# Normalising before the split, statistics by halves, and PSUM read directly: a two-layer encoder on one core

## What is computed

```python
def rms_norm(x, g):
    y = xf * lax.rsqrt(jnp.mean(xf * xf, axis=-1, keepdims=True) + EPS)
    return (y * g).astype(x.dtype)

def conv_ffn(h, w_up, conv_w, conv_b, w_down):
    z = causal_dwconv(h @ w_up, conv_w, conv_b)      # width 3, depthwise
    g, u = jnp.split(z, 2, axis=-1)
    return (jax.nn.silu(g) * u) @ w_down

# layer 0: x += rglru_sgu_mixer(rms_norm(x));  x += conv_ffn(rms_norm(x))
# layer 1: x += chunk_band_attention(rms_norm(x));  x += conv_ffn(rms_norm(x))
# out = rms_norm(x)
```

## Time and profile before

| | |
|---|---|
| runs shown | 1182.83, 1182.06, 1182.88 us; median 1182.83 us |
| span of the profiled execution | 1180.5 us |
| TensorE busy | 1130.1 us, 96% |
| VectorE busy | 729.0 us, 62% |
| ScalarE busy | 440.7 us, 37% |
| GpSimd busy | 474.2 us, 40% |
| mean granted clock of TensorE | 0.985 of full speed |

### The profile page before, as it was taken

The page is one execution under the profiler, slowest core; times in us unless marked ns, Lnnn a source line. Parts: engine busy times, 40 slices in busy tenths (PEclk is TensorE's granted clock), DMA queues, the critical chain, the costliest instruction groups (busy, mean ns, idle before and its releaser), DMA issues.

```text
span 1180.5 us, 15574 instructions
## 1 busy us (share of the span) xinstructions
PE 1130.1 (96%) x5215; PEld 920.4 (78%) x5215; DVE 729.0 (62%) x1155; ACT 440.7 (37%) x674; POOL 474.2 (40%) x210
## 2 busy tenths in 40 slices
PE   7998799999999999999999999989999999999996
PEld 5886578888888887788777777768888888887886
DVE  5879866766666752223777777675766767651123
ACT  5283343332322332223455555544323223232221
POOL 4343443444444444443332222143544444444442
PEclk8998899999999999999999999999999999999998
DMA  7372222332322332332323222122323232233302
GB/s 267 104 227 72 71 89 72 109 106 89 103 92 95 100 104 96 103 107 89 107 72 103 77 71 75 51 72 72 125 89 107 89 99 97 91 105 107 100 25 72
DMA packets 37587, 115.08 MB, mean 97 GB/s; under 512 B 4752, under 2 KB 7440, under 8 KB 37552
## 3 DMA queue, kind: packets, MB, share of 16 engines
q1 hardware_dynamic: 35376, 110.41, 28.0%
q10 hardware_dynamic: 2176, 4.19, 1.1%
HBM read 112.19 MB, written 6.59 MB: 101 GB/s over the span
## 4 chain that ended last, share of the span: by engine, by line
PE 75%; DVE 7%; issue 5%; ACT 3%; DVEq 0%; ACTq 0%
PE bank L1120 24%; PE bank L1121 23%; PE bank L1122 23%; PE bank L1413 1%; PE bank L1430 1%; DVE p_sb L1029 1%; PE bank L1428 1%; DVE acc L728 1%; ACT p_sb L614 1%; PE bank L1311 1%; DVE o_sb L1046 1%; ACT o_sb L639 0%; DVE x L1112 0%; ACT oh L647 0%; DVE small L1026 0%
## 5 line engine op out<-in xcount | busy, mean ns | idle before, releaser
L358 POOL TENSOR_TENSOR wl<-raw,wh 128x1024 fp32r<-128x1024 f32 x191 | 463.8, 2430 | 679.0 <-ACT wh L413 679.0
L1120 PE MATMUL bank<-xh,wh 128*128 128x512 f32 x1008 | 401.4, 398 | 7.4 <-DVE xl L721 6.6
L1121 PE MATMUL bank<-xl,wh 128*128 128x512 f32 x1008 | 394.0, 391 | 0.0
L1122 PE MATMUL bank<-xh,wl 128*128 128x512 f32 x1008 | 394.0, 391 | 0.0
L413 ACT ACTIVATE wh<-raw 128x1024 fp32r<-128x1024 f32 x191 | 202.0, 1059 | 384.9 <-PE bank L1122 339.1
L1120 PEld LDWEIGHTS bank<-xh,wh 128*128 128x128 f32 x1008 | 190.3, 189 | 51.5 <-DVE xl L721 7.3
L1122 PEld LDWEIGHTS bank<-xh,wl 128*128 128x128 f32 x1008 | 190.2, 189 | 40.6
L1121 PEld LDWEIGHTS bank<-xl,wh 128*128 128x128 f32 x1008 | 190.5, 189 | 36.9
L1120 PE MATMUL bank<-ah,wh 128*128 128x512 f32 (+1 forms) x357 | 136.2, 381 | 0.0
L1121 PE MATMUL bank<-al,wh 128*128 128x512 f32 (+1 forms) x357 | 134.4, 376 | 0.0
L1122 PE MATMUL bank<-ah,wl 128*128 128x512 f32 (+1 forms) x357 | 134.4, 376 | 0.0
(11 more groups left out here) (193 smaller groups left out, 1131.7 us busy)
## 6 DMA issues: line engine op xcount, KB each, us to landing
raw<-weights SPq DMA_DIRECT2D x191, 512.0 KB, 3.3
bias_scratch<-ext_scratch SPq DMA_DIRECT2D x1, 4096.0 KB, 19.0
bias<-bias_scratch ACTq DMA_DIRECT2D x8, 512.0 KB, 3.6
x<-x_in SPq DMA_DIRECT2D x8, 256.0 KB, 5.4
out<-x SPq DMA_DIRECT2D x4, 384.0 KB, 3.0
raw<-weights SPq DMA_DIRECT2D x2, 256.0 KB, 3.4
out<-x SPq DMA_DIRECT2D x2, 256.0 KB, 2.2
lng<-ln_g SPq DMA_DIRECT2D x1, 256.0 KB, 9.9
```

Of the source, the lines that this page charges most:

```text
L358: nc.gpsimd.tensor_tensor(wl[:, c % RING].rearrange("p k c -> p (k c)"), raw[:, c % RAW], wh[:, c % RING].rearrange("p k c -> p (k c)"), A ...
L1120: nc.tensor.matmul(dst, w_hi_part, m_hi, start=first, stop=False)
L1121: nc.tensor.matmul(dst, w_hi_part, m_lo, start=False, stop=False)
L1122: return nc.tensor.matmul(dst, w_lo_part, m_hi, start=False, stop=last)
```

## The change

- **Norms 1 to 3.** The last tiles of the residual stage (three in stages 0 and 2, one in stage 1; `TAIL`) are computed as two halves of 256 positions, all of half 0 first, then half 1. Their weight units are released only in half 1. The statistics of half 0 are made between the matmuls of half 1, those of half 1 between the first matmuls of the next stage.
- **Normalise first, split then.** VectorE forms x times gain times rstd (rstd read from PSUM) into a ring of four half tiles `xn` (`scale_tile`), ScalarE copies the high part (`half_hi`), VectorE subtracts for the low part (`half_lo`). `xh` and `xl` are now normalised, and rstd is no more applied behind matmuls.
- **Opening.** `opening_units` takes the first *three* units of the next stage by halves: half 0 of all three, then half 1 k by k, so that all three are released at its end.
- **FFN.** ScalarE forms the first tap out of PSUM (`tap`), VectorE adds the two others reading the bank (`conv`); the bank is free only after that (`conv_done`). `ub` goes. One bank (3) holds SiLU and product.
- **Attention.** High and low part of q and k are made straight from the bank; v is copied by ScalarE. `qkv_evacuate` goes. A bank is free when the low part is made.

The diff, cut to its core:

```diff
 # VectorE
+            def scale_tile(norm, half, m):
+                if m == 0:
+                    dve.wait_ge(spread_mm, STAT_BASE[norm] + half + 1)
+                if n >= 4 or norm > 1:
+                    dve.wait_ge(x_lo, X_BASE[norm] + n - 3)
+                stt(xn[:, m % 4], x[:, m, cols], gain(norm, m), bank[HALF_STAT_BANKS[half]][:, 0:HALF],
+                    ALU.mult, ALU.mult).then_inc(x_norm, 1)
+            def half_lo(norm, half, m):
+                dve.wait_ge(x_hi, X_BASE[norm] + KT * half + m + 1)
+                tt(xl[:, m, cols], xn[:, m % 4], xh[:, m, cols], ALU.subtract).then_inc(x_lo, 1)
...
+                tail(0, 1)
+                half_statistics(norm, 0)
+                square_part(stage, KT)
+                scale_tile(norm, 0, 0)
+                scale_tile(norm, 0, 1)
+                half_lo(norm, 0, 0)
+                tail(1, 1)
+                scale_tile(norm, 0, 2)
+                half_lo(norm, 0, 1)
+                scale_tile(norm, 0, 3)
+                half_lo(norm, 0, 2)
+                tail(2, 1)
+                scale_tile(norm, 0, 4)
+                half_lo(norm, 0, 3)
+                scale_tile(norm, 0, 5)
+                half_lo(norm, 0, 4)
+                half_statistics(norm, 1)
+                scale_tile(norm, 0, 6)
+                half_lo(norm, 0, 5)
+                scale_tile(norm, 0, 7)
+                half_lo(norm, 0, 6)
+                scale_tile(norm, 1, 0)
+                half_lo(norm, 0, 7)
...
-                    tt(u[:, 2:], bank[UP_BANKS[t % 6]][:], rstd[:], ALU.mult).then_inc(up_free[layer], 1)
-                    link(ts(c[:], u[:, 2:2 + T], tap[2], tap[3], ALU.mult, ALU.add))
-                    link(stt(c[:], u[:, 1:1 + T], tap[1], c[:], ALU.mult, ALU.add))
-                    stt(c[:], u[:, 0:T], tap[0], c[:], ALU.mult, ALU.add).then_inc(conv_done[layer], 1)
+                    link(stt(c[:, 1:T], bank[b][:, 0:T - 1], tap[1], c[:, 1:T], ALU.mult, ALU.add))
+                    stt(c[:, 2:T], bank[b][:, 0:T - 2], tap[0], c[:, 2:T], ALU.mult, ALU.add).then_inc(conv_done[layer], 1)
...
 # ScalarE, residual_tiles
+                half_root(norm, 0)
+                item_square(stage, KT)
+                split_hi(first_unit + KT)
+                half_hi(norm, 0, 0)
+                half_hi(norm, 0, 1)
+                item_square(stage, KT + 1)
+                split_hi(first_unit + KT + 1)
+                half_hi(norm, 0, 2)
+                half_hi(norm, 0, 3)
+                item_square(stage, KT + 2)
+                split_hi(first_unit + KT + 2)
+                half_hi(norm, 0, 4)
+                half_root(norm, 1)
...
 # TensorE
+OPEN_ORDER = [(0, 0), (0, 1), (0, 2), (1, 0), (1, 1), (1, 2), (0, 3), (1, 3), (0, 4), (1, 4), (0, 5), (1, 5),
+              (0, 6), (1, 6), (0, 7), (1, 7)] + [(2, k) for k in range(KT)]
+                for n, (u, k) in enumerate(OPEN_ORDER):
+                    if k == 0:
+                        pe.wait_ge(w_lo, unit + u + 1)
+                    if u == 0:
+                        pe.wait_ge(x_lo, X_BASE[norm] + k + 1)
+                    step(u, k, 0)
+                    if n == 5:
+                        half_statistics(stage, 1)
+                    elif n == 13:
+                        half_spread(norm, 1)
+                for k in range(KT):
+                    pe.wait_ge(x_lo, X_BASE[norm] + KT + k + 1)
+                    for u in range(3):
+                        ins = step(u, k, 1)
+                        if k == KT - 1:
+                            ins.then_inc(w_used, 1)
```

More of the change, by code:

```diff
@@ L470, in _ @@
             split_hi(U_AX + 3)
[L471 removed]
+            statistics()
             for m in range(MT_A):
@@ L910, in residual_tiles, with whole @@
             def residual_tiles(first_unit, stage):
-                for m in range(KT):
-                    dve.wait_ge(w_used, first_unit + m + 1)
-                    tt(x[:, m], x[:, m], bank[RES_BANKS[stage][m]][:], ALU.add).then_inc(x_ready, 1)
-                    norm_tile(stage + 1, m, m % 2)
-                statistics(stage + 1)
+                def whole(n):
+                    dve.wait_ge(w_used, first_unit + n + 1)
+                    residual_add(stage, n, bank[RES_BANKS[stage][n]][:])
@@ new lines, in tail @@
+                def tail(m, half):
+                    n = KT - 3 + 3 * half + m
+                    if half:
+                        dve.wait_ge(w_used, first_unit + KT - 2 + m)
+                    else:
+                        dve.wait_ge(tail_mm, m + 1 + (4 if stage else 0))
+                    add_part(stage, n, bank[TAIL_BANKS[stage][half][m]][:, 0:HALF])
+                    if not (half == 1 and m == 0):
+                        square_part(stage, n)
+                norm = stage + 1
@@ new lines, in residual_tiles @@
+                for n in range(KT - 3):
+                    whole(n)
+                for m in range(3):
+                    tail(m, 0)
+                tail(0, 1)
[8 more added lines that the diff above has]
+                scale_tile(norm, 0, 3)
@@ L999, in qk_split_lo @@
                 hi, lo = (kh, kl) if which else (qh, ql)
-                tt(lo[:], (k_sb if which else q_sb)[:], hi[:], ALU.subtract).then_inc(qk_lo, 1)
+                ps = bank[proj_bank(c, turn, which)]
+                stt(lo[:], ps[:], 1.0 if which else -(HD ** -0.5), hi[:], ALU.mult, ALU.subtract).then_inc(qk_lo, 1)
             def scores(c, turn, g):
@@ L1356, in final_spread @@
             def final_spread(half):
-                pe.wait_ge(col_done, 5 + half)
-                for j in range(2):
-                    r = rstd_col[:, 2 * half + j:2 * half + j + 1]
-                    ins = nc.tensor.matmul(bank[FINAL_STAT_BANKS[half]][:, P * j:P * j + P],
-                                           r.to_broadcast([P, P]), ident[:], start=True, stop=True)
-                ins.then_inc(spread_mm, 1)
+                half_spread(4, half)
             ffn(0)
```

430 lines of the change are left out of this document (278 added, 152 removed).

## The result

The changed kernel takes 1221.33 us, the median of four runs from 1215.96 to 1223.62; the kernel before takes 1182.86 us (1182.06 to 1183.16). The ratio is 1.0325, 95% interval 1.0306 to 1.0343: 38.5 us slower. 25.1 us slower was forecast, with a range to 1224. So sign and range held, and a third of the loss was missing from the sum.

A forecast was written before the change was run, and what follows sets the result against it. TensorE's queue of products plus its few stalls was taken as the bound. Sum: 1182.8 + 0.4 - 7.8 - 2.3 - 2.1 + 5.8 + 5.8 + 3.2 + 22.1 = 1207.9 us, range 1182 to 1224.

The forecast's parts named there:

- rival C: FFN up phase goes at ScalarE's rhythm, 42 pairs lose 21 us: 1229 us; chance 0.08.
- Openings, +22.1 forecast: First products of each stage wait for normalised low parts, some held beside weight subtractions: 22.1 us more.
- The walk: Openings' engines laid side by side step by step: waits of 7.2 us for stages 0 and 2, 7.7 for stage 1.
- Rival A: Openings' collisions fall the other way, GpSimd waits instead of VectorE: openings cost 4.5 us, total 1188.7; chance 0.22.
- Refill, +5.8 and +3.2: At each FFN's start TensorE waits 2.9 us for weights, slots being released late; clock falls add 1.6 each.
- Halves, +5.8: In tails and openings, 142 products computed as two halves cost 0.04 us more each; 5.8 us with shorter statistics.
- Start of attention, -2.3: The 2.78 us wait for kl shrinks to 1.5 us without losing the clock: 2.3 us less.
- residual adds, -2.1: The low part no longer stands between residual adds, so two waits go: 2.1 us less.
- FFN, +0.4: FFN convolution with one gate bank: only the first down product waits, at most 0.2 us per FFN.
- the chain of 5.3 us: FFN pair's work from weight copy to low part after its second unit, 5.3 us, covered by a 5.44 us unit.
- Attention pairs, -7.8: After the softmax VectorE goes to ql at once, 1.3 us less in each of six pairs: 7.8 us less.
- rival D: Attention pairs wait as before, or q's high copy comes no earlier: 1215.7 us; chance 0.56 together with the forecast.

The follow-up runs named there:

- e1: Changed kernel with GpSimd's subtraction for the openings' nine weight units cut to 8 columns instead of 1024 and its loop written out: 1202.5 us, ratio 1.0169.
- e10: Kernel before, with weight unit 3 copied behind the transposed tiles and GpSimd's subtractions in two pieces: 1159.6 us, ratio 0.9824.
- e5: Kernel before, with weight unit 3 copied behind the transposed tiles and GpSimd's subtractions in quarters: 1155.3 us, ratio 0.9773.
- e11: Kernel before, with weight unit 3 copied behind the transposed tiles and GpSimd's subtractions in eight pieces: 1155.1 us, ratio 0.9777.
- e2: Changed kernel with half 1 of an opening computed unit by unit instead of k-tile by k-tile: 1211.2 us, ratio 1.0228.
- e9: Kernel before, with 80 of the 86 FFN up units computed as two halves of 256 positions: 1208.9 us, ratio 1.0236.
- e3: Kernel before, with ScalarE's copy of weight unit 3 moved behind the transposed tiles: 1171.1 us, ratio 0.9903.
- e7: Changed kernel with ScalarE's copy of weight unit 3 moved behind the transposed tiles: 1211.2 us.
- e8: Changed kernel with half 1 by units, subtractions in quarters, unit 3 copied behind the transposed tiles, and down projection begun in bank 4: 1177.3 us, ratio 0.9957.
- e4: Changed kernel with each GpSimd subtraction cut into four of 256 columns: 1194.2 us, ratio 1.0113.

## Why the prediction was right, and where it was not

**What bounds the kernel: right.** 137 us less work of VectorE and a longer kernel. In the up phases TensorE had no gap in either trace; rival C did not come.

**Openings, +22.1 forecast.** The mechanism was right by the place of each wait; the sizes were off. The waits are 15.0 us (5.3, 5.9 and 3.8 for the three), not 22.1. The walk put the subtractions 4.8 us apart and they came 4.5 apart; for the first opening it had waits of 2.3, 0.3, 1.9, 1.4 and 1.0 us with 0.3 at the spread, and they are 1.88, none, 1.52, 1.01, 0.91 and none. For the second it had 1.1, 4.4, 1.2 and 0.9, and they are 1.16, 3.81, none and 0.91. The third repeats the first, but while the clock was low TensorE came late to low 4 and did not wait for it. But the clock, which stood in the bounds and not in the value, fell in all three: windows of 2 us give 1.7, 3.4 and 1.7 us, 6.8 in all. 15.0 + 6.8 = 21.8. The total agrees by two errors that cancel, which is luck; and 0.9 us of the 6.8 fell while TensorE was waiting anyway. e1 shows the cause of one half: held low parts make 7.7 of the 15.0 us, and 7.3 stay without them, where the prediction had 4.5 for the chain alone. Rival A is out: each held low part had started behind GpSimd (187.20 against 186.73), and those that started some 0.26 us ahead of it passed in 0.42 us.

The Trainium skill (SBUF - State Buffer, Who interferes with whom) states the rule behind it: an operation of VectorE with two SBUF inputs contends with a GpSimd instruction that reads SBUF, one with at most one SBUF input does not unless it runs in a 2-port mode, which `tensor_scalar` can enter, and the order of issue decides who blocks, for the whole instruction. The traces agree: 2.19 us for a low part from two SBUF tensors, 0.48 us for a scale with PSUM beside the same subtraction, and the longest held operations of e10 and e5 shrink with the GpSimd instruction; the one row of e11 does not agree. They also show where the prediction's class, "operations that read two SBUF tensors", was too narrow: the softmax step is a `tensor_scalar` that reads one SBUF tensor, and it is held for as long (below).

**Refill, +5.8 and +3.2.** The wait is 2.92 us at both FFNs, as worked out to the hundredth; e2 removes it. The clock fell behind the first (1.7 us) and not behind the second: 1.7 of 3.2.

**Halves, +5.8: right** (5.9 by e9). The 1 us that the figure of the Trainium skill (TensorE: Matmul & The Clock Gate, Back-to-back issue gap) for a lone matmul gives is refuted: e9 has 0.039 to 0.041 us a product of three where that figure has 0.0075.

**Start of attention, -2.3, and residual adds, -2.1: right.** The waits there are 1.29 us for kl and 1.02 us for the next pair's first weight unit, without the fall of the clock that came behind the 2.78 us; 2.78 + 1.6 - 1.29 - 1.02 = 2.1 less.

**FFN, +0.4: mis-sized.** The wait for the last low part was put at 0.2 us and is 0.94, twice. The step that failed is the chain of 5.3 us. It measures 5.89, from the weight copy at 429.76 to the end of the low part at 435.65: the tap, taken from a plain copy of the same size (0.60), takes 0.76 us with scale and shift, and handovers between engines of some 0.4 us were left out. Then the matmul starts 0.45 us behind the low part, where in the openings it starts 0.05 us behind; this wait stands ahead of a loop of the program, and that entering it takes the 0.4 us is likely and not shown.

```profile
430.73 0.76 ACT L569 ACTIVATE cu<-bank,par 128x512 f32<-128x512 f32 x1
...
434.96 0.69 DVE L1074 TENSOR_TENSOR al<-bank,ah 128x512 f32 x1 [0.89 <-ACT ah L585]
...
436.10 0.47 PE L1244 MATMUL bank<-ah,wh 128*128 128x512 f32 x1 [0.94 <-DVE al L1074]
```

**Attention pairs, -7.8: wrong.** A pair went from 26.7 to 26.3 us, 2.4 us in six. The step that failed reads "VectorE goes to ql at once: 0.68 + 0.63 = 1.3 us less, under the mean wait of 8.3 / 6 = 1.4 us". It shortened the piece that follows the softmax's last steps, and that piece was not what set the pair. The sign that was named, a wait for the low part under 0.4 us, came true (that wait, 8.3 us in six, is gone from the list), and most of the time stayed, because the wait moved to another place. This is rival D, "the pairs wait as before", for 5.4 of its 7.8 us; the high copy of q does come earlier. D's 1215.7 us is also the time of the profiled execution, 1216.0, but that is chance, as the sum below shows. A pair of the changed kernel:

```profile
651.06 2.37 POOL L334 TENSOR_TENSOR wl<-raw,wh 128x1024 fp32r<-128x1024 f32 x1 [7.60 <-ACT wh L388]
...
651.21 2.37 DVE L1162 TENSOR_SCALAR p_sb<-p_sb,small 128x256 f32<-128x256 f32 x1
...
653.71 1.09 PE L1578 MATMUL bank<-ident,p_sb 128*128 128x128 f32 x8 [1.31 <-DVE p_sb L1162]
```

In the kernel before, too, the softmax had two steps of 256 columns at its end; the first passed in 0.35 us, begun 0.07 us ahead of the subtraction, the second was held 2.28 us, and TensorE could begin its transposes behind the first half. After the change the subtraction starts 0.15 us ahead of the *first* of the two steps, and TensorE waits 1.3 us in front of the transposes instead of 1.5 behind them. The kernel before:

```profile
627.21 0.35 DVE L1029 TENSOR_SCALAR p_sb<-p_sb,small 128x256 f32<-128x256 f32 x1
...
627.28 2.52 POOL L358 TENSOR_TENSOR wl<-raw,wh 128x1024 fp32r<-128x1024 f32 x1 [7.83 <-ACT wh L413]
```

The prediction named this risk as a bound ("if the softmax step and its subtraction shift against each other", 4 us) and did not go below it. What it should have asked is why a step of 256 columns takes 2.28 us in the earlier trace rows, and what the wait there becomes once ql is out of it. e3 and e7 settle it: the held step is the cause, in both kernels, and moving one copy is worth 11.3 and 10.1 us.

**The sum.** By these sizes the profiled execution gives 15.0 + 6.8 + 5.8 + 1.7 + 5.9 + 1.9 - 2.4 - 2.1 - 2.1 = 30.5 us of 33.6. Against the forecast, +25.1, the pairs make the largest difference (5.4 us more), then the FFN (1.5 more) and the refill's clock (1.5 less). The remaining 3 us are not measured piece by piece, but a wait costs TensorE more than the list of waits says: the listed time begins at the end of the last matmul's way through the array, which is 0.16 us behind the start that the pace would have given the next one (0.39 - 0.23, and 0.28 - 0.12 for halves), and the second matmul behind a wait starts 0.33 us after the first, not 0.23. That is 0.27 us a wait, by estimate 3.5 us for 15 new ones less the two that went.

**The 5 us between this execution and the median** go with the clock. The four runs have spans of 1214.1, 1217.5, 1221.1 and 1221.5 us at mean granted clocks of 0.981, 0.977, 0.974 and 0.974, so span times clock is 1191, 1189.5, 1189.4 and 1189.8 us: the same work at a lower clock. The same goes for e1 (0.984 with 1200.9 us, 0.979 with 1206.8 and 1207.6) and e2 (0.982 with 1204.3, 0.971 and 0.973 with 1213.2 and 1213.9). Behind which waits the clock fell in the three slower runs of the changed kernel is not known, as only the fastest was profiled.

**What stays open.** e8 and e5 have the same cures and differ by 22.0 us. The halves make 5.9 of them. e8's waits in the openings are 8.8 us for low parts and 1.5 for weights, and its clock fell in two of them (1.7 us each by windows of 2 us); that makes some 20. No run separated normalising first from the halves, so it wasn't tried whether the chain alone, on whole tiles, would cost more or less.

## What to carry to other kernels

VectorE was busy 62% of the time beside a TensorE at 96%, and taking work from it was worth nothing, but *when* its operations met GpSimd's was worth 2.3%: look for operations of one shape with two durations, and ask what runs beside the long ones. Two small cures, a copy moved behind the critical steps and long GpSimd instructions cut in four, brought 27.7 us, while the large restructuring cost 38.5. When a step is cut out of a chain in front of a wait, follow the waiting engine to its previous dependence: if that one is late too, the wait only moves forward.

Here the factor applied behind the matmul was hidden work; applied ahead of it, it needs its statistics first and puts a chain through three engines in front of the first product.

## What the runs showed of the hardware that was not expected

- A GpSimd subtraction of 1024 columns takes 2.43 us; in pieces of 512, 256 and 128 columns each takes 1.37 (e10), 0.78 to 0.81 (e4, e5) and 0.50 us (e11). A piece costs about 0.2 to 0.3 us beyond its columns, which paid down to 256.
- A VectorE step that reads one SBUF tensor can be held, too: the softmax step of 256 columns took 0.35 us, and 2.28 to 2.49 us in six places beside a subtraction in each of the two kernels.
- The fall of the clock from 2.4 to 1.2 GHz came with single waits of 2.3 to 3.8 us or clusters of shorter ones, but not always: behind 2.92 us it fell at the first FFN's refill and not at the second's, in the same execution; at the wait of 2.3 us for weights in attention's output product it fell in e3 and not in the kernel before.
- A product in halves costs the same in a long stream (0.041 us) as in one tile (0.038 by the pace), so the cost is that of the matmuls. In half 1 of an opening, where the bank changes with every product, the pace of the halves is the same 0.120 us (206.12 to 207.20, nine matmuls).
